# A decoder layer with 32 experts on one Trainium2 core: expert weights in a ring of four slot pairs, gate and up loaded whole, down multiplied between them

## What is computed

```python
def expert_step(acc, args):                      # 32 experts, one after the other
    wg, bg, wu, bu, wd, bd, cw = args            # each matrix 1024 x 1024, float32 (4 MB)
    g = jnp.minimum(xt @ wg + bg, SWIGLU_LIMIT)
    u = jnp.clip(xt @ wu + bu, -SWIGLU_LIMIT, SWIGLU_LIMIT)
    y = ((u + 1.0) * g * jax.nn.sigmoid(SWIGLU_ALPHA * g)) @ wd + bd
    return acc + cw[:, None].astype(y.dtype) * y, None
```

## Time and profile before

| | us |
|---|---|
| median of three runs (1140.16 to 1141.27) | 1140.3 |
| the profiled execution, as timed | 1143.17 |
| its span in the trace | 1141.4 |
| TensorE busy | 1095.7 (96%) |
| VectorE busy | 405.2 (36%) |
| ScalarE, GpSimd busy | 175.1 (15%), 89.8 (8%) |
| all DMA | 438.88 MB, mean 384 GB/s |

### The profile page before, as it was taken

The page is one execution under the profiler, slowest core; times in us unless marked ns, Lnnn a source line. Parts: engine busy times, 40 slices in busy tenths (PEclk is TensorE's granted clock), DMA queues, the critical chain, the costliest instruction groups (busy, mean ns, idle before and its releaser), DMA issues.

```text
span 1141.4 us, 14558 instructions
## 1 busy us (share of the span) xinstructions
PE 1095.7 (96%) x5749; PEld 516.9 (45%) x5749; DVE 405.2 (36%) x964; ACT 175.1 (15%) x366; POOL 89.8 (8%) x89
## 2 busy tenths in 40 slices
PE   8999999999999999999999999999999999999997
PEld 7879899843334333333333333333333333333333
DVE  5773666532223322222322222222222222222222
ACT  5545665400000000000000000000000000000000
POOL 2226447000000000000000000000000000000000
PEclk9999999999989999999999999999999999999999
DMA  8955723999999999999999999999999999999996
GB/s 299 333 213 201 242 75 127 425 383 424 427 416 409 428 427 429 429 427 429 428 428 429 428 429 429 427 429 429 428 429 428 428 429 427 429 428 425 429 428 272
DMA packets 50252, 438.88 MB, mean 384 GB/s; under 512 B 6594, under 2 KB 12806, under 8 KB 24870
## 3 DMA queue, kind: packets, MB, share of 16 engines
q1 hardware_dynamic: 50166, 438.23, 92.8%
q10 hardware_dynamic: 48, 0.13, 0.0%
HBM read 437.30 MB, written 1.05 MB: 384 GB/s over the span
## 4 chain that ended last, share of the span: by engine, by line
PE 64%; DMA 33%; ACT 1%; DVE 0%; issue 0%; POOL 0%; POOLq 0%; SPq 0%; DVEq 0%
PE bank L1871 35%; DMA ring<-in_w_e_up_dram 18%; DMA ring<-in_w_e_gate_dram 12%; PE bank L1844 3%; PE bank L1892 3%; DMA ring<-in_w_e_down_dram 3%; PE bank L1860 2%; PE bank L1483 2%; PE bank L1633 1%; PE bank L1634 1%; PE bank L1635 1%; PE bank L1912 1%; PE bank L1492 1%; PE bank L1494 1%; PE bank L1493 1%; PE bank L1486 1%
## 5 line engine op out<-in xcount | busy, mean ns | idle before, releaser
L1871 PE MATMUL bank<-ring,heads 128*64 128x512 f32 x3004 | 678.9, 599 | 14.7 <-DMA ring<-in_w_e_gate_dram 13.2
L1871 PEld LDWEIGHTS bank<-ring,heads 128*64 128x64 f32 x3004 | 204.0, 137 | 420.8 <-issue 376.0
L1413 DVE TENSOR_TENSOR x<-x,bank 128x512 f32<-128x512 f32 x124 | 79.9, 684 | 144.8 <-PE bank L1892 144.8
L1361 DVE TENSOR_SCALAR heads<-bank 128x512 f32<-128x512 f32 x32 | 22.1, 691 | 289.5 <-PE bank L1871 289.5
L881 ACT ACTIVATE work<-bank 128x256 f32<-128x256 f32 x32 | 12.3, 385 | 493.0 <-PE bank L1905 493.0
L696 POOL TENSOR_TENSOR x<-x,heads 128x256 f32<-128x256 f32 x2 | 1.4, 726 | 914.3 <-ACT heads L915 914.3
L1892 PE MATMUL bank<-heads,work 64*128 64x512 f32 x248 | 72.5, 642 | 0.0
L402 POOL TENSOR_TENSOR w_lo<-ring,w_hi 128x1024 fp32r<-128x1024 f32 (+1 forms) x35 | 65.3, 1890 | 53.9 <-ACT w_hi L720 53.9
L720 ACT ACTIVATE w_hi<-ring 128x512 fp32r<-128x512 f32 (+2 forms) x84 | 58.8, 729 | 25.7 <-PE bank L1722 7.4
L1844 PE MATMUL bank<-work,xn 128*128 128x128 f32 x480 | 58.5, 275 | 0.0
L1844 PEld LDWEIGHTS bank<-work,xn 128*128 128x128 f32 x480 | 56.0, 192 | 0.0
(11 more groups left out here) (317 smaller groups left out, 972.4 us busy)
## 6 DMA issues: line engine op xcount, KB each, us to landing
ring<-in_w_e_gate_dram SPq DMA_DIRECT2D x61, 2048.0 KB, 31.2
ring<-in_w_e_up_dram SPq DMA_DIRECT2D x61, 2048.0 KB, 32.4
ring<-in_w_e_down_dram SPq DMA_DIRECT2D x60, 2048.0 KB, 32.1
ring<-in_w_in_dram SPq DMA_DIRECT2D x8, 2048.0 KB, 9.1
ring<-in_w_e_down_dram SPq DMA_DIRECT2D x8, 1024.0 KB, 17.7
spare<-in_w_e_gate_dram SPq DMA_DIRECT2D x1, 4096.0 KB, 18.4
ring<-in_w_out_dram SPq DMA_DIRECT2D x2, 2048.0 KB, 8.0
ring<-in_w_e_up_dram SPq DMA_DIRECT2D x4, 1024.0 KB, 6.7
```

Of the source, the lines that this page charges most:

```text
L1361: nc.vector.tensor_scalar(e_g, banks[1][:, :], LIMIT, None, ALU.min).then_inc(g_made, 1)
L1413: ins = nc.vector.tensor_tensor(x[:, t, 512 * h:512 * h + 512], x[:, t, 512 * h:512 * h + 512], bank67[:, j % 2, :], ALU.add)
L1871: last = mm(bank[C * half:C * half + C, :], lhs(kk), kept_row[half] if kept else w[:, k, 512 * half:512 * half + 512], start=(kk == 0 and ...
```

## The change

The ring becomes four pairs of neighbouring slots, used in the order `PAIR_ORDER`; matrix n of the new order (gate e, down e - 1, up e) goes into pair n % 4. In the loop, gate and up are each one load of 4 MB with rows of 32 KB, issued when the matrix that was in the pair is used up; down stays two loads of 2 MB, issued together. Experts 1 to 3 still load by halves, each as the same half of the older matrix is used. The products come in the order gate, down of the expert in front, up; in even experts the gather stands before the gate; the scatter of t = 0 stands in the middle of up half 0 (`between`). VectorE keeps the gathered rows first in even experts. The last expert keeps its order.

```diff
-EX_ORDER = (7, 3, 6, 4, 5, 0, 1, 2)
-EX_SLOTS = len(EX_ORDER)
+PAIR_ORDER = (3, 2, 1, 0)
+EX_SLOTS = 2 * len(PAIR_ORDER)
...
-        BODY = [("gate", 0, 0), ("down", 0, 1), ("down", 1, 1), ("gate", 1, 0), ("up", 0, 0), ("up", 1, 0)]
...
+        def place_of(m, u):
+
+            return {"gate": 3 * u - 1, "up": 3 * u + 1, "down": 3 * u + 3}[m]
...
+        def slots_of(n):
+            pair = PAIR_ORDER[n % len(PAIR_ORDER)]
+            return 2 * pair, 2 * pair + 1
...
+        FIRST_USED = [("gate", 0), ("up", 0), ("gate", 1)]
+        INTO_USED = [("up", 0, 1), ("gate", 0, 2), ("up", 1, 1)]
...
+            def load_matrix(m, e, n):
+
+                s = slots_of(n)[0]
+                src = a[ex_src[m]][0, bass.ds(e, 1)].rearrange("o (p k) n -> p (o k n)", p=P)
+                sp.dma_start(ring[:, s:s + 2, :].rearrange("p s n -> p (s n)"), src).then_inc(ring_in[s], 16)
...
+            def first_experts():
+
+                def as_freed(m, e, of, done):
+
+                    for h in range(2):
+                        sp.wait_ge((half_done, mat_done)[h][of], done)
+                        load_half(m, h, e, place_of(m, e))
+                sp.wait_ge(*low_done(OUT))
+                load_half("gate", 1, 1, place_of("gate", 1))
+                sp.wait_ge(y_made, KD)
+                load_half("gate", 0, 0, 0)
...
+                load_by_halves()
+                load_half("gate", 0, 1, place_of("gate", 1))
+                for i in range(len(INTO_USED)):
+                    load_as_used(i)
+                sp.wait_ge(mat_done["up"], 1)
+                load_half("gate", 1, 2, place_of("gate", 2))
+                as_freed("down", 1, "gate", 2)
+                as_freed("up", 2, "down", 1)
+                as_freed("gate", 3, "up", 2)
+                as_freed("down", 2, "gate", 3)
+                as_freed("up", 3, "down", 2)
...
+                if not (last and u == 0):
+                    sp.wait_ge(mat_done["up"], prev)
+                    load_matrix("gate", e, place_of("gate", u))
+                if ends:
...
+                    return
+                sp.wait_ge(mat_done["gate"], now)
+                for h in range(2):
+                    load_half("down", h, e_before, place_of("down", u - 1))
+                sp.wait_ge(mat_done["down"], prev)
+                load_matrix("up", e, place_of("up", u))
...
             sp.wait_ge(mat_done["up"], last_step)
-            load_quarters(0)
-            sp.wait_ge(half_done["gate"], total)
-            load_quarters(1)
+            for h in range(2):
+                load_quarters(h)
...
+                if not first and u % 2 == 0:
+                    keep_x(it, u)
                 if not first:
                     keep_hT(it)
-                if not first and not ends:
+                if u % 2 and not ends:
                     keep_x(it, u)
...
                 for k in range(4):
                     kk = 4 * h + k
+                    if between and k == 2:
+                        between()
...
                 if u % 2 == 0:
                     pe.wait_ge(ex_made, it - 1)
+                    gather(None, 1, False)
                 pe.wait_ge(g_made, it)
                 product("gate", 0, banks[1], x_of(u), it, base, u, False, in_last)
                 turn_h(it)
-                if u % 2 == 0:
-                    gather(None, 1, False)
-                elif u % 2:
+                if u % 2:
                     gather(it + 3, 0, True)
                 turn_hot(it)
+                if u % 2 == 0:
+                    pe.wait_ge(ex_made, it)
+                product("gate", 1, banks[1], x_of(u), it, base, u, False, in_last)
                 pe.wait_ge(ehT_made, it)
                 product("down", 0, banks[3], h_of, it - 1, base, u - 1, False, in_last)
                 product("down", 1, banks[3], h_of, it - 1, base, u - 1, False, in_last)
-                if u % 2 == 0:
-                    pe.wait_ge(ex_made, it)
-                product("gate", 1, banks[1], x_of(u), it, base, u, False, in_last)
-                scatter(it - 1, 0, isinstance(it, int) and it == 3)
-                product("up", 0, banks[2], x_of(u), it, base, u, False, in_last)
-                scatter(it - 1, 1, isinstance(it, int) and it == 3)
+                product("up", 0, banks[2], x_of(u), it, base, u, False, in_last,
+                        lambda: scatter(it - 1, 0, with_biases))
+                scatter(it - 1, 1, with_biases)
                 product("up", 1, banks[2], x_of(u), it, base, u, False, in_last)
```

More of the change, by code:

```diff
@@ L331, in build @@
         ]
-        BY_HALVES = [0, 1]
         in_ring = [b[0] for b in BLOCKS if b[0] != "cv1"]
@@ L1846, in gather, with product @@
                 last.then_inc(gathered, 1)
-            def product(m, h, bank, lhs, it, base, u, first=False, in_last=False, place=None):
-                place = ex_place(m, h, u, first) if place is None else place
-                if in_last and place in LEFT_OUT:
+            def product(m, h, bank, lhs, it, base, u, first=False, in_last=False, between=None):
+                n = 0 if first and m == "gate" else place_of(m, u)
+                if in_last:
+                    n = LAST_PLACE.get((m, u), n)
+                if in_last and (m, u) == ("gate", 0):
                     pe.wait_ge(spare_in, 16)
@@ L1862, in product @@
                     kk = 4 * h + k
-                    if not first and isinstance(base, int) and k == 2 and place - EX_SLOTS in range(len(second_in)):
-                        pe.wait_ge(second_in[place - EX_SLOTS], 16)
+                    if between and k == 2:
+                        between()
+                    if not first and isinstance(base, int) and k == 2 and (m, h, u) in INTO_USED:
+                        pe.wait_ge(second_in[INTO_USED.index((m, h, u))], 16)
                     if first and m == "gate":
@@ L1973, in _ @@
             it = last_base + u
+            LAST_ORDER = [(m, h, back) for m, back in (("gate", 0), ("up", 0), ("down", 1)) for h in range(2)]
             def last_piece(i):
-                m, h, back = LAST_BODY[i]
+                m, h, back = LAST_ORDER[i]
                 bank, rows = {"gate": (banks[1], x_of(u)), "up": (banks[2], x_of(u)), "down": (banks[3], h_of)}[m]
-                product(m, h, bank, rows, it - back if back else it, last_base, u - back, False, True, len(BODY) * u - 2 + i)
+                product(m, h, bank, rows, it - back if back else it, last_base, u - back, False, True)
             pe.wait_ge(g_made, it)
```

142 lines of the change are left out of this document (64 added, 78 removed).

## The result

The changed kernel takes **1147.8 us** (median of 5 runs, 1147.0 to 1152.0) beside 1140.4 us (1140.2 to 1141.3) of the kernel before: ratio 1.0071, interval 1.0050 to 1.0091. The forecast was 1143.0 us, 0.2% slower, with a range up to 1147.5: right in sign, too small, and out of the range by 0.3 us in the first series. One execution of the kernel before, in the first series of experiments, took 1848.0 us at a granted clock of 0.555 and is left out everywhere; all others stand.

A forecast was written before the change was run, and what follows sets the result against it. Weight transfers bound the middle, TensorE's work after expert 27's up weights land the end. Terms 2.3 - 2.9 + 5.9 - 2.6 = +2.7 us on the median 1140.3 gave 1143.0 us; own range 1141 to 1146, whole range 1138.0 to 1147.5.

The forecast's parts named there:

- Edit 1: Gate and up loads with 32 KB rows: 0.06 us saved a matrix over 48 matrices, -2.9 us (0 to -4.3).
- (b): Rival: 32 KB rows run faster in a steady stream than in `spare`'s stretch, 1136.7 us at 437 GB/s; chance 0.20.
- (d): Rival: the 32 KB rows don't help at all, 1145.9 us; chance 0.05.
- Edit 2: Slot pair refilled only when its whole matrix is used: stream runs dry at expert 3, +2.3 us (-0.6 to +3.5).
- the fixed 2.65 us: Part of a load's landing time on a nearly empty queue that isn't transfer, added to gate 5 around 340 us.
- Before this point ... nothing changes: Experts 1 to 3 still go by halves with the issues at the times of before, so no change there.
- Edit 3: TensorE waits for whole matrices: +5.9 us in the open at expert 27, -2.6 us of tail waits returned.
- Edit 4: New order of products and loads: same TensorE instructions, each wait covered, 0 us.
- (a): Rival: expert 3's stall isn't exposed, as the scatters' new place keeps the clock up; 1140.1 us, chance 0.17.
- (c): Rival: 2.4 us waits before up products drop the clock, 1.0 to 1.7 us each, open at expert 27; 1144.7, chance 0.08.

The follow-up runs named there:

- e14: Changed kernel without the biases' eight products, each 4 MB load issued as two 2 MB loads with 16 KB rows, products waiting for both: 1144.0 us, 1.0023.
- e6: Changed kernel without the eight products that add the down projections' biases in expert 3's scatters: 1140.2 us, 0.9991.
- e1: Changed kernel with each 4 MB load issued as two 2 MB loads with 16 KB rows, products still waiting for both: 1149.7 us, 1.0063.
- e9: The changed kernel as it stands, run again in a later series: 1146.5 us, 1.0043.
- e2: e1 with each half of a product waiting only for its own half: 1144.3 us, 1.0027.
- e3: e2 with each 2 MB load issued when its half of the slot pair has been used: 1141.2 us, 0.9993.
- e15: e14 with each half of a product waiting only for its own half: 1140.6 us, 0.9992.
- e16: e15 with every 2 MB load issued when its half of the slot pair has been used: 1141.0 us, 0.9992.
- e5: Kernel before, without the eight products that add the down projections' biases in expert 3's scatters: 1140.8 us, 0.9995.
- e12: Kernel before with the biases' eight products moved to the scatters of experts 5 and 6, experts 4 to 7 written out for TensorE: 1141.2 us, 1.0003.
- e4: Changed kernel with every fourth expert's up matrix (7 to 27) as two 2 MB loads, each product half waiting for its own: 1146.8 us, 1.0046.
- e7: Changed kernel with experts 4 to 7 loaded and waited for in halves, each issued as its half of the pair is used: 1143.7 us, 1.0028.
- e8: Changed kernel with the edits of e7 and e4 together: 1141.3 us, 1.0006.
- e10: e7 with the biases' products moved to experts 5 and 6, and up matrices of the last two experts of each four in halves: 1142.2 us, 1.0011.
- e11: Changed kernel with the biases' eight products moved to the scatters of experts 5 and 6, experts 4 to 7 written out: 1142.4 us, 1.0013.
- e13: e10 with gate matrices of the last two experts of each four also as two loads with half waits: 1141.2 us, 1.0000.

## Why the prediction was too low

**Edit 1, the rows: right, low by 0.02 us a matrix.** Forecast -2.9, period 29.2, 430 to 431 GB/s. Measured without disturbance -3.7 (e14 to e6), period 29.21, so 0.08 us a matrix instead of 0.06, within my 0 to 0.09. Rivals (b), rows faster still, and (d), no gain, fall. The estimate by the Trainium skill (DMA: Bandwidth & Descriptors, Why small descriptors are slow), 0.03 us a matrix, is under half of what is measured. The Trainium skill's ceiling of 435 GB/s (DMA: Bandwidth & Descriptors, Specifications) was not reached in the steady stretch, at 430 to 431. With the biases in place the gain may be smaller: e1 to the changed kernel gives -2.3 to +0.9, from different series and each give or take some 2 us, so this isn't shown by times. A part of it is in the traces: from gate 5's issue to up 5's landing e1 takes 34.6 us (337.20 to 371.80) and the changed kernel and e9 36.0, so with the queue dry the 4 MB loads lose 1.4 us.

**Edit 2, refilling by pairs: the step that failed.** I had "+2.3 us". It is 3.9 by e2 and e3, and 0 without the biases' products (e15, e16). Its place, expert 3 at 340 us, and its kind, an issue that comes when the queue has run dry, were right. Three things in its working were wrong.
First, the hole itself. SyncE's issue of up 4 in the changed kernel, and its time to landing:

```profile
316.90 0.33 SPq L491 DMA_DIRECT2D ring<-in_w_e_up_dram  x1
```

```profile
ring<-in_w_e_up_dram SPq DMA_DIRECT2D x1, 4096.0 KB, 18.7
```

Up 4 lands at 335.6, so from there to up 5 at 372.52 it is 36.9 us for transfers of 29.2: 7.7 us are lost. My working has 337.6 to 370.1, so 3.3 lost; before lost some 1. I put the fixed 2.65 us on gate 5 and 0.5 us behind it. In the trace gate 5 lands 14.0 us after up 4, 4.3 more than its transfer instead of 2.7: the queue had been empty for 0.9 us when it was issued, and the load took 13.1 us where I had 12.4. Down 4 was issued at 346.69, 2.9 us ahead of gate 5's landing at 349.61, and its first half landed 7.3 us after that instead of 4.9; up 5, issued some 8.4 us ahead of down 4's landing, took 10.7 instead of 9.7. So two more gaps follow the first, 2.4 and 1.0 us.
Second, "Before this point ... nothing changes". The stream of the changed kernel was 2.0 us ahead of before's at up 4 (335.6 against 337.6). This head start hid part of the first error: up 5 is 2.4 us later than forecast and not 4.4. That is luck, not working.
Third, the baseline. I took the profiled execution of before with its half clock and its hole as the usual one, and added the difference to a median 2.9 us lower. The median of before doesn't pay that hole (e5, e12), so in most executions there was no old loss to take off from the new one.
Half clock makes this term vary: up 5 landed at 369.2 with full clock (e9), at 372.5 with half clock from 327.5 to 336, and at 377.9 in e4, whose loads are the same up to there. It isn't all of the changed kernel's wide scatter (8 us over its eleven runs, 1143.7 to 1152.0), as e7 and e8 scatter by 8.2 and 7.8 us with nothing freed in pairs at expert 3. What the wide scatter needs is the biases' products (e6: 1.9 us; e14: 2.7); the rest of its cause is open.

**Edit 3, waiting for whole matrices: right.** Forecast 5.9 - 2.6 = +3.3. Measured 3.5 (e14 to e15), 4.1 (e1 to e2), and 3.7 in the first pair of traces (130.9 against 127.2 us from the landing to the end). From up 27's product to expert 28 the changed kernel takes 1025.10 - 1015.24 = 9.86 us (forecast 9.71), and from there to the end 121.0 against 123.4, so 2.4 came back (forecast 2.6). The slip at expert 28 was 7.1 us instead of 5.3, 1.7 of the 1.8 from the later landing (1015.2 instead of 1013.5). What I had not seen is that the wait binds at gate 27 as well once up 27 is repaired (e10).

**Edit 4, the order: right**, 0 forecast, -0.8 give or take 1.0 with the biases (e3) and -0.3 without.

With the biases in place the four terms as measured are 3.9 for pairs, 4.1 for whole-matrix waits, -0.8 for the order, and -2.3 to +0.9 for the rows: 4.9 to 8.1 us, where I had 2.7. The pairs' term is the largest of the misses that a pair of experiments in one series shows; the rows' term is the least certain.

**Rivals.** (a), the clock kept up at expert 3, happens in some executions (e9's and e7's profiled ones); even then freeing in pairs left a hole in e9, and that execution took 1146.2 us and not (a)'s 1140.1. (c), the clock falling behind the waits, is true in its mechanism, and in some executions its price is paid. In the loop the falls hide in the slack, as the prediction has it, and each fall shortens the next expert's wait to 0.5 to 0.7 us. So what (c) costs hangs on whose turn it is at expert 27. In the changed kernel's first trace, and in those of e6 and e14, its wait was a short one and nothing fell (130.9 us from the landing to the end each). In e9's trace, and in e1's, it was 2.25 and 2.33 us, the clock fell, and 1.6 us were paid (132.5 and 132.6 us), within (c)'s 1.0 to 1.7. How many executions pay it isn't shown. From e14 to e15, where e14's trace has no fall at expert 27, the dips of the loop vanish, and the 3.5 us gained are the whole-matrix wait at up 27 by the landings, with nothing left for the loop.

## What to carry to other kernels

Before a buffer's refill is made coarser, look for the longest step between two frees, not the mean one: here 4 us of extra products in one of 32 experts cost nothing with fine refills and half-matrix waits and 6 to 9 us with coarse ones, and keeping the refills fine there (e7, 1.7 to 4.9 us back) or moving the work (e11, 3.4 to 6.6) gives most of it back. A hole in a short queue cost more here than the late issue, for the loads issued into the short queue behind it lost time again. A wait that lowers the clock can eat its own slack and shorten the next one, so that costs alternate from step to step; look at several steps and several executions before saying whether the last one pays. Make the sum against several executions or the median, never against the state of the one that was profiled, where that one contains an event (here half clock) that may be rare before and common after.

## What the runs showed of the hardware

- TensorE's clock fell to 1.2 GHz while the engine was busy without a gap: the stretches from 300 to 340 us show no idle time (30.00 of 30.00 and 10.00 of 10.00 us busy), and products take nearly twice as long from 327.5 to 336 us. What it did before was products of 32 and 64 rows, sixteen of them between 319 and 330.5 us, with eight of 128 rows between them. The same program kept 2.4 GHz there in another execution (0.75 against 1.00 in 330 to 340 us). Without the eight products of 32 rows no profiled execution showed it at this place (e5, e6, e14, e15, e16: 1.00 in 310 to 350 us); moved to experts 5 and 6, they brought it there in three of four (0.94 in 370 to 400 us in e10, e12 and e13, 1.00 in e11).
- The clock fell right behind a wait of 2.19 us (eight products in 3.33 us for 1.94) and behind one of 2.20 us in e10 (5.35 for 3.65), though TensorE had been busy up to the wait. It did not fall behind every such wait: in the changed kernel's loop behind 8 of 10 of 2.2 us, in e9 behind 8 of 11, and behind none of the shorter ones (0.5 to 1.5 us). Where no wait was longer than 1.3 us (e2), it stayed at 1.00 in the loop.
- A matrix of 4 MB in 32 KB rows takes 9.71 us in a full queue against 9.79 for two loads of 2 MB (periods of 29.21 and 29.37 us), and 430 to 431 against 428 GB/s over 600 us.
- In the changed kernel's trace a load issued 2.9 us ahead of the landing of the one before it cost 2.4 us more than its transfer, one issued 8.4 us ahead still 1.0. This is no rule by distance: in before's trace a load issued 4.8 us ahead lost only 0.2 (issued at 337.65, landed 9.9 us later, the one before it at 342.5).
